# Five edits of order on TensorE, VectorE and ScalarE in a two-layer streaming trunk on one core

## The chip, the core and the metric

The kernel runs on one core of one Trainium2 chip. Its time is the device time of one execution in microseconds (us). Five engines of the core work side by side, each through its own list of instructions in order: TensorE (PE in the profile; its weight loads are shown apart as PEld), VectorE (DVE), ScalarE (ACT), GpSimd (POOL) and SyncE (SP). They wait for one another by semaphores that count up. A lower time is better.

## The reference, cut to what matters

The input is 512 frames of 1024 numbers. Layer 0 has two kinds of attention side by side, layer 1 a gated recurrence; behind each stands a feed-forward part with a convolution of width 3, and a last norm closes the trunk. Every input of a mixer or a feed-forward part is first normed and then shifted and scaled by vectors computed from the condition `c`.

```python
for l in range(DEPTH):                                  # DEPTH = 2
    mod = cond @ ada_w[l] + ada_b[l]
    sh1, sc1, g1, sh2, sc2, g2 = jnp.split(mod, 6, axis=-1)
    h = modulate(rms_norm(x, norm_mix_g[l]), sh1, sc1)
    y = stick_window_mixer(h, ...) if l % 2 == 0 else hgrn2_mixer(h, ...)
    x = x + g1[:, None, :] * y
    h = modulate(rms_norm(x, norm_ffn_g[l]), sh2, sc2)
    x = x + g2[:, None, :] * conv_ffn(h, ...)           # ((gelu(conv(h Wg))) * (h Wu)) Wd
return rms_norm(x, final_g)

# sliding-window heads of layer 0 (8 of them), per block of 128 queries:
m = max(max(logits), sink)
p = exp(logits - m)
out = (p / (sum(p) + exp(sink - m))) @ v
```

## The kernel before, in words

**Products in three parts.** The big products are made to float32 accuracy from parts of lower precision. Each operand is split into a high part (ACT rounds it: `w_hi`, `hT_hi`) and a low part (DVE subtracts: `w_lo`, `hT_lo`), and TensorE adds three matmuls in one PSUM bank: high weights by high input, high weights by low input, low weights by high input. A *unit* is a block of weights of 1024 columns: for each of the 8 chunks k of the input it has these three matmuls of 128x512, 24 in all. SP loads a unit into one of two slots, ACT and DVE split it, TensorE uses it (`unit`, line 1626).

**Pairs of units.** Behind a norm the chunks of the input come one by one, so the first two units behind it run as a pair (`unit_pair`, line 1648): chunk k of the first unit, and two chunks later (`LAG`) that of the second. The first unit waits at each chunk for `h_lo`, which DVE counts up when the chunk's low part is done; ACT counts `h_hi` for the high part. There are four such calls: the output projection of layer 0 (`U_OUT0`), the feed-forward parts of both layers (`U_FFN0`, `U_FFN1`) and the input projection of layer 1 (`U_IN1`). The last three stand right behind a norm, whose chunks DVE makes by lines 1056 (normed and scaled) and 1062 (low part) in turn, with ACT's line 653 (high part) between them.

**Opening.** The first four units run as a `quad` over half of the chunks, then over the other half. Between the two halves TensorE transposes columns of the input x (`x_columns`), makes the sums of the second half of the first condition vectors (`first_sums(1)`, 16 matmuls of one column), transposes two more columns, and issues four dummy matmuls whose result nobody reads (`keep_clock`).

**Window heads ("band heads").** The 8 sliding-window heads of layer 0 go through three pairs of PSUM banks in turn: `window_logits` (PE), `window_max` (DVE), `window_exp` (ACT), `window_norm` (DVE), `window_transposes` (PE), `window_copy` (the first bank of the pair by ACT, line 750, the second by DVE, line 1238), `window_values` (PE, into `obank`), `window_out` (DVE, line 1243, after each second head). ACT counts its copies in `pt_act`, DVE in `pt_dve`. Head 7's part of the loop also holds chunks 0 and 1 of the pair `U_OUT0`, which writes to the banks `proj`, the pair of banks of heads 0, 3 and 6.

**Second half of the last product.** `down(1)` makes the last product in two halves of 11 units. When the first half is out, DVE scales its columns (`final_scale`, line 1400), and TensorE transposes them (`final_transposes`, 16 transposes) behind the first unit of the second half; ACT copies one bank of them away (line 889). Eight units in a loop and two last ones (`last_two`) follow.

Everything here is set by the order in which the lines are written out; there is no scheduler. Two lines that decide a step below:

```python
1923                    window_values(h - 1)                                  # h = 7
1924                    unit_pair(U_OUT0, h_base["o0"], range(0, 2))
```

Of the kernel before, what the change touches and what calls it, by code (L numbers as in the profile page):

```python
# [31 lines left out]
P = 128  # L32
SEQ = 512
D = 1024
DC = D // P
# [52 lines left out]
U_OUT0 = U_IN0 + len(UNITS0)  # L88
# [7 lines left out]
HALF = FB // 2  # L96
# [62 lines left out]
def trunk(nc, x, c, ada_w, ada_b, norm_mix_g, norm_ffn_g, ab_w_in, ab_sinks, ab_w_out, hg_w_in,  # L159
          hg_lb_gamma, hg_onorm_g, hg_w_out, ffn_w_gate, ffn_w_up, ffn_conv_w, ffn_conv_b,  # L160
          ffn_w_down, final_g, tables, level_masks, out):
    with ExitStack() as ctx:
# [435 lines left out]
        def _(act):  # L598
# [8 lines left out]
            def split(u, slot):  # L607

                if isinstance(u, int) and u < 4:
                    act.wait_ge(raw_in[slot], 32 * (u // 2 + 1))  # L610
                else:
                    act.wait_ge(raw_in[slot], u * 8 + (48 - 8 * slot))
                if isinstance(u, int) and u < 4:
                    dst = (w_hi[:, slot, :], quad_hi[slot])[u // 2]
                else:
                    dst = w_hi[:, slot, :]
                    if isinstance(u, int) and u < 6:
                        act.wait_ge(quad_half, 1)
                    else:
                        act.wait_ge(unit_mm, u - 1)  # L620
                nc.scalar.activation(dst, w_raw[:, slot, :], ACT.Copy).then_inc(hi_done, 1)  # L621
# [256 lines left out]
            def down(u0, n, last=False):  # L878
                act.preload_act_table_set(EXP_LN_SET)
                with act.Fori(0, HALF // 2) as i:  # L880
                    for s in range(2):
                        split(u0 + 2 * i + (2 + s), s)
                for q in range(4):
                    squares(n, q)
                split(u0 + HALF + 1, 0)
                split(u0 + HALF + 2, 1)
                if last:
                    act.wait_ge(misc_full, MISC_AT["fin"] + 1)
                    nc.scalar.activation(out_nat[:, TB - 1, 0:512], misc[:], ACT.Copy).then_inc(misc_free, 1)
                with act.Fori(0, HALF // 2 - 1) as i:  # L890
                    for s in range(2):
                        split(u0 + HALF + 3 + 2 * i + s, s)
                for q in range(4, DC):
                    squares(n, q)
                if not last:
                    split(u0 + FB, 0)
                    split(u0 + FB + 1, 1)
                    root(n)
                    modulated(n)
# [107 lines left out]
        def _(dve):  # L1007
# [207 lines left out]
            def window_max(h):  # L1215
                s = h % 3
                for b in range(TB):
                    z, lo, _, n = window_block(b, s)
                    dve.wait_ge(sw_full, 2 * h + 1 + b // 2)
                    link(nc.vector.tensor_reduce(soft[:, s, 3, b:b + 1], z[:, lo:lo + n], AX.X, ALU.max))  # L1220
                nc.vector.tensor_scalar(soft[:, s, 0, :], soft[:, s, 3, :], sinks[:, h:h + 1], -1.0,
                                        ALU.max, ALU.mult).then_inc(max_done, 1)

            def window_norm(h):
                s = h % 3
                dve.wait_ge(p_done, h + 1)
                link(nc.vector.tensor_tensor(soft[:, s, 3, :], soft[:, s, 1, :], soft[:, s, 2, :], ALU.add))
                link(nc.vector.reciprocal(soft[:, s, 2, :], soft[:, s, 3, :]))
                for b in range(TB):
                    _, _, at, n = window_block(b, s)  # L1230
                    nc.vector.tensor_scalar(p_bufs[s][:, at:at + n], p_bufs[s][:, at:at + n],
                                            soft[:, s, 2, b:b + 1], None, ALU.mult).then_inc(p_norm, 1)

            def window_copy(h):
                dve.wait_ge(pt_full, 2 * h + 2)
                if h >= 3:
                    dve.wait_ge(pv_done, SB_HEADS + h - 2)
                nc.vector.tensor_copy(pt_bufs[h % 3][:, 384:896], pairs[h % 3][1][:]).then_inc(pt_dve, 1)
# [67 lines left out]


            window_norm(1)
            window_max(2)
            split(U_OUT0 + 1, 1)  # L1310
            window_copy(0)
            for h in range(1, SW_HEADS):
                window_copy(h)
                if h + 1 < SW_HEADS:
# [285 lines left out]
        def _(pe):  # L1600
# [50 lines left out]
            def unit_pair(u, h_from, ks=range(DC)):  # L1651


                parts_ready(u + 1)
                steps = [(k, 0) for k in ks] + [(k, 1) for k in ks]
                for k, s in sorted(steps, key=lambda step: step[0] + LAG * step[1]):
                    if s == 0:
                        pe.wait_ge(h_lo, h_from + k + 1)
                    at = slice(k * P, (k + 1) * P)
                    mm(proj[s][:], w_hi[:, s, at], hT_hi[:, k, :], start=(k == 0))  # L1660
                    mm(proj[s][:], w_hi[:, s, at], hT_lo[:, k, :])
                    last = mm(proj[s][:], w_lo[:, s, at], hT_hi[:, k, :], stop=(k == DC - 1))
                    if k == DC - 1:
                        last.then_inc(unit_mm, 1)
                    elif s == 0 and k == DC // 2 - 1:
                        last.then_inc(pair_half, 1)
# [120 lines left out]
            keep_clock(proj[0], 5)  # L1787
            quad(0)
            x_columns(range(3, 6))
            pe.wait_ge(first_used, 2 * DC)  # L1790
            misc_wait("first1")
            first_sums(1)
            x_columns(range(6, DC))
            pe.wait_ge(x_new, 6)
            keep_clock(zb[3], 4)

            def tile_in(b):

# [117 lines left out]
            for h in range(1, SW_HEADS):  # L1916
                if h < SW_HEADS - 1:
                    window_transposes(h)
                    window_values(h - 1)
                    if h + 2 < SW_HEADS:  # L1920
                        window_logits(h + 2)
                else:
                    window_values(h - 1)
                    unit_pair(U_OUT0, h_base["o0"], range(0, 2))
                    window_transposes(h)

            unit_pair(U_OUT0, h_base["o0"], range(2, 4))
# [31 lines left out]
            def down(layer, u0, n):  # L1959
# [64 lines left out]
                pe.wait_ge(gp_lo, FB * (layer + 1))  # L2024
                last_two(u0 + HALF - 2, 1, FB - 4, down_banks[0])
                one(u0 + HALF, 1, 0, first=True, mod_group=(8, None)[layer], banks=down_banks[1])
                if layer:
                    pe.wait_ge(fin_y, 4)
                    pe.wait_ge(gap_free, len(GAP_MODS))
                    misc_wait("fin")  # L2030
                    final_transposes(0, range(TB - 1), range(4)).then_inc(fin_full, 1)
                    final_transposes(0, range(TB - 1, TB), range(4)).then_inc(misc_full, 1)
                with pe.Fori(0, HALF // 2 - 1) as i:
                    for s in range(2):
                        one(u0 + HALF + 1 + 2 * i + s, s, 4 * i + 2 * s + 2, banks=down_banks[1])
                last_two(u0 + FB - 2, 0, FB - 4, down_banks[1])
                if not layer:
                    norm_sum(n)
# [124 lines left out]
```

## Time and profile before

| what | value |
|---|---|
| median of 3 runs | 1359.72 us (1358.35 to 1359.87) |
| the profiled execution, its own time | 1360.04 us |
| its span, first to last instruction | 1358.2 us |
| TensorE matmul busy in the span | 1323.5 us (97%) |
| TensorE weight loads busy | 1083.0 us (80%) |
| DVE, ACT, POOL busy | 808.7, 558.1, 46.9 us |
| mean granted TensorE clock | 0.993 |

The page gives one execution. Busy time is time in instructions; in a row of the timeline the bracket tells how long the engine had been idle before it and what released it. A row that ends in x4 stands for four instructions of the same kind in a run. PEclk is the granted TensorE clock as a share of 2.4 GHz: 1.00 or, at the lower of its two levels (1.2 GHz), 0.50.

### The profile page before, as it was taken

The numbers are of one execution on the slowest core, as the hardware profiler recorded it, in microseconds if no ns is written. First come the engines' busy times: TensorE is split into PE (matmuls) and PEld (weight loads), VectorE is DVE, ScalarE is ACT, GpSimd is POOL, SyncE is SP. The second block draws the span as 40 slices with busy tenths as digits, with TensorE's granted clock in tenths as the row PEclk, the third lists the DMA queues.
The fourth block names the chain that finished last, engine by engine and source line by source line (L and its number), as shares of the span: only waits on it lengthen the run. The fifth ranks groups of instructions, "written<-read, shape, count | busy, mean of one in ns | idle before, by whom it ended". The sixth has DMA issues, their size and how long they took to land.

```text
span 1358.2 us, 17432 instructions
## 1 busy us (share of the span) xinstructions
PE 1323.5 (97%) x6281; PEld 1083.0 (80%) x6281; DVE 808.7 (60%) x1197; ACT 558.1 (41%) x837; POOL 46.9 (3%) x92
## 2 busy tenths in 40 slices
PE   6999998899999999999999999999999999999998
PEld 5877776777888888888778888888788888888786
DVE  5745557567666656436697777775765455552423
ACT  6656554334333333212255555553343333332212
POOL 1000000000000000001100000000000000000000
PEclk9999999999999999999999999999999999999998
DMA  9543431153544555465622222224523333332232
GB/s 336 167 124 109 125 109 32 46 164 103 150 142 143 150 146 147 141 184 190 210 82 78 76 65 63 74 67 125 155 78 95 105 93 93 94 107 93 82 100 81
DMA packets 190148, 160.38 MB, mean 118 GB/s; under 512 B 5271, under 2 KB 163176, under 8 KB 190098
## 3 DMA queue, kind: packets, MB, share of 16 engines
q1 hardware_dynamic: 177696, 116.34, 28.5%
q0 software_dynamic: 11856, 42.68, 10.4%
q8 instruction: 32, 0.52, 0.2%
q10 hardware_dynamic: 546, 0.69, 0.1%
q14 instruction: 18, 0.15, 0.0%
HBM read 157.59 MB, written 2.10 MB: 118 GB/s over the span
## 4 chain that ended last, share of the span: by engine, by line
PE 89%; DVE 5%; ACT 2%; SPq 1%; issue 1%; DMA 1%; DVEq 0%; ACTq 0%
PE proj L1603 61%; PE z L1603 22%; PE obank L1603 3%; PE misc L1603 2%; SPq L479 1%; DVE ada_sum L1118 1%; DMA w_raw<-ab_w_in 1%; DVE normed L1056 0%; ACT w_hi L621 0%; DVE hT_lo L1062 0%; SPq L489 0%; DVE soft L1220 0%; ACT q_sb L741 0%; DVE w_lo L1018 0%; DVE xT L1410 0%
## 5 line engine op out<-in xcount | busy, mean ns | idle before, releaser
L1603 PE MATMUL proj<-hT_hi,w_hi 128*128 128x512 f32 x1112 | 441.5, 397 | 4.6 <-DVE hT_lo L1062 4.1
L1603 PE MATMUL proj<-hT_hi,w_lo 128*128 128x512 f32 x1112 | 433.7, 390 | 0.0
L1603 PE MATMUL proj<-hT_lo,w_hi 128*128 128x512 f32 x1112 | 433.4, 390 | 0.0
L1018 DVE TENSOR_TENSOR w_lo<-w_raw,w_hi 128x1024 fp32r<-128x1024 f32 x189 | 231.2, 1224 | 338.6 <-ACT w_hi L621 338.6
L621 ACT ACTIVATE w_hi<-w_raw 128x1024 fp32r<-128x1024 f32 x191 | 202.0, 1059 | 442.7 <-PE proj L1603 261.2
L1603 PEld LDWEIGHTS proj<-hT_hi,w_hi 128*128 128x128 f32 x1112 | 209.2, 188 | 57.2 <-DVE hT_lo L1062 8.0
L1603 PEld LDWEIGHTS proj<-hT_hi,w_lo 128*128 128x128 f32 x1112 | 209.0, 188 | 44.4
L1603 PEld LDWEIGHTS proj<-hT_lo,w_hi 128*128 128x128 f32 x1112 | 209.3, 188 | 43.3 <-issue 1.7
L1603 PE MATMUL z<-gated_hi,w_hi 128*128 (+1 forms) x264 | 104.5, 396 | 0.2 <-DVE xT L1410 0.2
L1603 PE MATMUL z<-gated_hi,w_lo 128*128 (+1 forms) x264 | 102.8, 389 | 0.0
L1603 PE MATMUL z<-gated_lo,w_hi 128*128 (+1 forms) x264 | 102.8, 389 | 0.0
L1165 DVE SCALAR_TENSOR_TENSOR ada_sum<-ada_raw,cond,ada_sum 128x1024 f32<-128x1024 f32 x70 | 89.6, 1280 | 2.5 <-DVE ada_sum L1165 0.5
L867 ACT ACTIVATE square<-square,small 128x512 f32<-128x512 f32 x44 | 31.9, 724 | 131.1 <-DVE square L1373 131.1
L567 POOL DMA_DIRECT2D ada_raw<-ada_w x80 | 42.4, 530 | 899.8 <-DVE ada_sum L1165 468.7
L1603 PEld LDWEIGHTS z<-gated_hi,w_hi 128*128 128x128 f32 x264 | 49.6, 188 | 10.4 <-DVE xT L1410 0.6
L1603 PEld LDWEIGHTS z<-gated_hi,w_lo 128*128 128x128 f32 x264 | 49.6, 188 | 10.4
L1603 PEld LDWEIGHTS z<-gated_lo,w_hi 128*128 128x128 f32 x264 | 49.6, 188 | 9.5
L1380 DVE TENSOR_TENSOR h<-proj,square 128x512 f32<-128x512 f32 x44 | 30.4, 691 | 23.6 <-PE proj L1603 22.4
L639 ACT ACTIVATE square<-xT 128x512 f32<-128x512 f32 x28 | 17.7, 632 | 52.0 <-DVE xT L1335 32.0
L1286 DVE SCALAR_TENSOR_TENSOR soft_a<-z,soft_a 128x128 f32<-128x128 f32 (+3 forms) x32 | 13.5, 483 | 37.3 <-ACT soft_a L800 37.3
L1373 DVE SCALAR_TENSOR_TENSOR square<-normed,small,square 128x512 f32<-128x512 f32 x44 | 33.1, 752 | 3.9 <-DVE square L1369 0.2
L1369 DVE SCALAR_TENSOR_TENSOR square<-normed,small,square 128x512 f32<-128x512 f32 x44 | 33.0, 751 | 3.9 <-DVE square L1366 0.2
(326 smaller groups left out, 1620.6 us busy)
## 6 DMA issues: line engine op xcount, KB each, us to landing
ada_raw<-ada_w POOLq DMA_DIRECT2D x80, 512.0 KB, 4.3
w_raw<-ffn_w_gate SPq DMA_DIRECT2D x44, 512.0 KB, 3.8
w_raw<-ffn_w_up SPq DMA_DIRECT2D x44, 512.0 KB, 3.9
w_raw<-ffn_w_down SPq DMA_DIRECT2D x44, 512.0 KB, 3.4
w_raw<-hg_w_in SPq DMA_DIRECT2D x32, 512.0 KB, 4.1
ada_first<-ada_w SPq DMA_DIRECT2D x16, 512.0 KB, 10.9
w_raw<-ab_w_in SPq DMA_DIRECT2D x14, 512.0 KB, 5.0
w_raw<-ab_w_out SPq DMA_DIRECT2D x8, 512.0 KB, 4.4
```

What stands on the lines that cost most here:

```text
L479: sp.dma_start(ada_first[:, DC * (1 - h) + k, :].rearrange("p (g n) -> p g n", g=2), src).then_inc(ada_first_in[h][k], 16)
L567: pool.dma_start(ada_raw[:, m % ADA_SLOTS, :], ada_w[layer].rearrange("(p k) n -> p k n", k=DC)[:, k, which * D:(which + 1) * D]).then_inc ...
L621: nc.scalar.activation(dst, w_raw[:, slot, :], ACT.Copy).then_inc(hi_done, 1)
L639: nc.scalar.activation(dst, xT[:, dc, :], ACT.Square).then_inc(sq_done, 1)
L867: nc.scalar.activation(square[:, 1, :], square[:, 0, :], ACT.Gelu_apprx_tanh, bias=conv_col(layer, 3, f)).then_inc(gelu_done, 1)
L1018: nc.vector.tensor_tensor(w_lo[:, slot, :], w_raw[:, slot, :], w_hi[:, slot, :].bitcast(F32), ALU.subtract).then_inc(lo_done, 1)
L1118: nc.vector.scalar_tensor_tensor(out=acc, in0=raw, scalar=scale, in1=acc, op0=ALU.mult, op1=ALU.add).then_inc(first_used, 1)
L1165: nc.vector.scalar_tensor_tensor(out=acc, in0=raw, scalar=scale, in1=acc, op0=ALU.mult, op1=ALU.add).then_inc(ada_used, 1)
L1369: nc.vector.scalar_tensor_tensor(out=square[:, 0, :], in0=normed[:, 0, 1:1 + SEQ], scalar=conv_col(layer, 1, f), in1=square[:, 0, :], op0= ...
L1373: nc.vector.scalar_tensor_tensor(out=square[:, 0, :], in0=normed[:, 0, 2:2 + SEQ], scalar=conv_col(layer, 2, f), in1=square[:, 0, :], op0= ...
L1380: nc.vector.tensor_tensor(h32[:, 0, :], proj[1][:], square[:, 1, :], ALU.mult).then_inc(gp_done, 1)
L1603: return nc.tensor.matmul(dst, weights_ap, moving, start=start, stop=stop, skip_group_check=True)
```

## The change

Five edits, all of them of order or of waits; no instruction is new but two dummy matmuls in the opening, and four dummies there go.

```diff
@@ ScalarE, down(): ACT's copy of the transposed bank goes behind the splits of the loop
+                with act.Fori(0, HALF // 2 - 1) as i:
+                    for s in range(2):
+                        split(u0 + HALF + 3 + 2 * i + s, s)
                 if last:
                     act.wait_ge(misc_full, MISC_AT["fin"] + 1)
                     nc.scalar.activation(out_nat[:, TB - 1, 0:512], misc[:], ACT.Copy).then_inc(misc_free, 1)
-                with act.Fori(0, HALF // 2 - 1) as i:
-                    for s in range(2):
-                        split(u0 + HALF + 3 + 2 * i + s, s)
@@ VectorE, window heads
             window_norm(1)
+            window_copy(0)
             window_max(2)
             split(U_OUT0 + 1, 1)
-            window_copy(0)
@@ TensorE, unit_pair()
+                    at = slice(k * P, (k + 1) * P)
+                    if s == 0:
+                        pe.wait_ge(h_hi, h_from + k + 1)
+                    mm(proj[s][:], w_hi[:, s, at], hT_hi[:, k, :], start=(k == 0))
+                    mm(proj[s][:], w_lo[:, s, at], hT_hi[:, k, :])
                     if s == 0:
                         pe.wait_ge(h_lo, h_from + k + 1)
-                    at = slice(k * P, (k + 1) * P)
-                    mm(proj[s][:], w_hi[:, s, at], hT_hi[:, k, :], start=(k == 0))
-                    mm(proj[s][:], w_hi[:, s, at], hT_lo[:, k, :])
-                    last = mm(proj[s][:], w_lo[:, s, at], hT_hi[:, k, :], stop=(k == DC - 1))
+                    last = mm(proj[s][:], w_hi[:, s, at], hT_lo[:, k, :], stop=(k == DC - 1))
@@ TensorE, opening
+            misc_wait("first1")
+            keep_clock(misc, 2)
             pe.wait_ge(first_used, 2 * DC)
-            misc_wait("first1")
             first_sums(1)
             x_columns(range(6, DC))
-            pe.wait_ge(x_new, 6)
-            keep_clock(zb[3], 4)
@@ TensorE, window heads, h = 7
+                    pe.wait_ge(pt_act, h)
+                    pe.wait_ge(pt_dve, h)
+                    unit_pair(U_OUT0, h_base["o0"], range(0, 2))
                     window_values(h - 1)
-                    unit_pair(U_OUT0, h_base["o0"], range(0, 2))
                     window_transposes(h)
@@ TensorE, down(): the loop goes ahead of the final transposes
+                with pe.Fori(0, HALF // 2 - 1) as i:
+                    for s in range(2):
+                        one(u0 + HALF + 1 + 2 * i + s, s, 4 * i + 2 * s + 2, banks=down_banks[1])
                 if layer:
                     pe.wait_ge(fin_y, 4)
                     pe.wait_ge(gap_free, len(GAP_MODS))
                     misc_wait("fin")
                     final_transposes(0, range(TB - 1), range(4)).then_inc(fin_full, 1)
                     final_transposes(0, range(TB - 1, TB), range(4)).then_inc(misc_full, 1)
-                with pe.Fori(0, HALF // 2 - 1) as i:
-                    for s in range(2):
-                        one(u0 + HALF + 1 + 2 * i + s, s, 4 * i + 2 * s + 2, banks=down_banks[1])
```

TensorE's row between the two halves of the opening quad (`z<-table,x_nat` are the transposes of x, `misc<-table,ada_sum` the one-column sums, `slope_r,ident_r` the dummies):

```order
-L1706 MATMUL z<-table,x_nat 128x128 x12
+L1708 MATMUL z<-table,x_nat 128x128 x12
+L1603 MATMUL misc<-slope_r,ident_r 128x512 x2
 L1603 MATMUL misc<-table,ada_sum 128x1 x8
-L1706 MATMUL z<-table,x_nat 128x128 x8
-L1603 MATMUL z<-slope_r,ident_r 128x512 x4
+L1708 MATMUL z<-table,x_nat 128x128 x8
 L1603 MATMUL z<-hT_hi,quad_w 128x512
```

Two dummies stand ahead of the sums, none ahead of the quad's second half.

VectorE's row where the window heads begin (the scalings of head 1, the copy of head 0 out of `proj`, the maxima of head 2, the split of a unit, the copy of head 1):

```order
 L1231 TENSOR_SCALAR soft_a<-soft_a,soft 128x128
 L1231 TENSOR_SCALAR soft_a<-soft_a,soft 128x256 x3
+L1238 COPY k_sb<-proj 128x512
 L1220 TENSOR_REDUCE soft<-z 128x1 x4
 L1221 TENSOR_SCALAR soft<-soft,sinks 128x4
 L1018 TENSOR_TENSOR w_lo<-w_raw,w_hi 128x1024
-L1238 COPY k_sb<-proj 128x512
 L1238 COPY pt_pair<-z 128x512
```

The copy of head 0 has gone ahead of four reductions, their maximum and one split.

TensorE's row at head 7, before (transposes of head 6, values of heads 5 and 6, chunks 0 and 1 of the pair, transposes of head 7):

```order
L1831 MATMUL proj<-table,q_sb 128x128 x7
L1603 MATMUL obank<-pt_pair,v_nat 64x128 x7
L1603 MATMUL obank<-k_sb,v_nat 64x128 x7
L1603 MATMUL proj<-hT_hi,w_hi 128x512
L1603 MATMUL proj<-hT_lo,w_hi 128x512
L1603 MATMUL proj<-hT_hi,w_lo 128x512
...
L1831 MATMUL z<-table,soft_a 128x128 x7
```

And now:

```order
L1832 MATMUL proj<-table,q_sb 128x128 x7
L1603 MATMUL obank<-pt_pair,v_nat 64x128 x7
L1603 MATMUL proj<-hT_hi,w_hi 128x512
L1603 MATMUL proj<-hT_hi,w_lo 128x512
L1603 MATMUL proj<-hT_lo,w_hi 128x512
...
L1603 MATMUL obank<-k_sb,v_nat 64x128 x7
L1832 MATMUL z<-table,soft_a 128x128 x7
```

The 12 matmuls of the pair have gone ahead of the values of head 6, and within each three the one with `hT_lo` is last.

## Rows read from the trace of the kernel before

**Rows 1.** The page: busy time and share of the span; then the chain's shares.

```profile
PE 1323.5 (97%) x6281; PEld 1083.0 (80%) x6281; DVE 808.7 (60%) x1197; ACT 558.1 (41%) x837; POOL 46.9 (3%) x92
PE 89%; DVE 5%; ACT 2%; SPq 1%; issue 1%; DMA 1%; DVEq 0%; ACTq 0%
```

**Rows 2.** Windows, 40 us of steady units: window, length, busy (instructions) per engine, PEclk, DMA.

```profile
320.00:360.00 40.00, 40.00 (x179) 33.10 (x178) 26.14 (x33) 15.29 (x20) 2.12 (x4) 1.00 0.55 158
```

**Rows 3.** Timeline of PE and ACT in the opening: start, us, instruction, [idle before].

```profile
41.03 1.95 PE L1603 MATMUL misc<-table,ada_sum 128*128 128x1 f32 x16 [0.53 <-DVE ada_sum L1118]
43.41 0.81 ACT L705 ACTIVATE hT_hi<-x_hat,mod,scale_g 128x512 fp32r<-128x512 f32 x1 [0.30 <-DVE scale_g L1129]
44.37 2.06 PE L1603 MATMUL z<-slope_r,ident_r 128*128 128x512 f32 x4
46.23 0.46 PE L1603 MATMUL z<-hT_hi,quad_w 128*128 128x512 f32 x1
```

**Rows 4.** Windows at both levels of the clock, columns as in rows 2.

```profile
18.00:22.00 4.00, 4.00 (x39) 4.00 (x38) 3.71 (x3) 3.87 (x8) 0.00 (x0) 1.00 1.09 360
43.00:46.00 3.00, 3.00 (x12) 2.71 (x12) 2.56 (x5) 2.70 (x5) 0.00 (x0) 0.50 0.61 175
...
218.00:246.00 28.00, 21.53 (x145) 17.59 (x143) 21.91 (x65) 14.56 (x55) 0.00 (x0) 1.00 0.00 1
248.00:251.00 3.00, 3.00 (x9) 2.23 (x8) 0.00 (x0) 0.00 (x0) 0.00 (x0) 0.50 0.00 0
```

**Rows 5.** Timeline of DVE, ACT and PE at the first window heads.

```profile
208.79 1.66 DVE L1220 TENSOR_REDUCE soft<-z 128x1 f32<-128x128 f32 x4
...
211.76 0.68 DVE L1238 COPY k_sb<-proj 128x512 f32<-128x512 f32 x1
...
212.46 0.30 ACT L743 ACTIVATE soft<-soft,sinks 128x4 f32<-128x4 f32 x1
...
212.54 2.23 PE L1603 MATMUL obank<-k_sb,v_nat 128*64 128x128 f32 x14 [2.63 <-issue]
...
212.96 0.15 DVE L1227 TENSOR_TENSOR soft<-soft 128x4 f32<-128x4 f32 x1
...
216.70 0.75 DVE L1220 TENSOR_REDUCE soft<-proj 128x1 f32<-128x128 f32 x2 [2.27 <-PE proj L1603]
...
219.27 0.37 ACT L741 ACTIVATE q_sb<-proj,soft 128x128 f32<-128x128 f32 x1 [5.61 <-DVE soft L1221]
```

**Rows 6.** Timeline of ACT and PE at heads 6 and 7.

```profile
243.97 0.49 ACT L750 ACTIVATE k_sb<-proj 128x384 f32<-128x384 f32 x1
...
246.35 1.91 PE L1603 MATMUL obank<-k_sb,v_nat 128*64 128x128 f32 x14 [3.44 <-DVE oT L1243]
248.20 0.80 PE L1603 MATMUL proj<-hT_hi,w_hi 128*128 128x512 f32 x1
...
252.41 0.93 PE L1831 MATMUL z<-table,soft_a 128*128 128x128 f32 x7
```

**Rows 7.** Waits of PE: engine line, waited for, us in total, times, longest.

```profile
PE proj L1603 <- DVE hT_lo L1062: 4.1, 9, 0.8
```

**Rows 8.** Timeline of ACT, DVE and PE, chunk 2 of the pair U_FFN0.

```profile
306.81 0.72 ACT L653 ACTIVATE hT_hi<-normed,mod 128x512 fp32r<-128x512 f32 x1 [0.94 <-DVE normed L1056]
...
308.14 0.75 DVE L1062 SCALAR_TENSOR_TENSOR hT_lo<-normed,mod,hT_hi 128x512 fp32r<-128x512 f32 x1
...
308.94 0.50 PE L1603 MATMUL proj<-hT_hi,w_hi 128*128 128x512 f32 x1 [0.49 <-DVE hT_lo L1062]
```

**Rows 9.** Timeline of DVE and PE between the halves of down(1).

```profile
1287.10 1.23 DVE L1018 TENSOR_TENSOR w_lo<-w_raw,w_hi 128x1024 fp32r<-128x1024 f32 x1 [0.26 <-ACT w_hi L621]
...
1287.52 0.39 PE L1603 MATMUL z<-gated_hi,w_lo 128*128 128x512 f32 x1
...
1289.96 1.09 PE L2013 MATMUL z<-table,ada_raw 128*128 128x128 f32 x8 [2.05 <-DVE ada_raw L1400]
```

## The prediction

> **What bounds the kernel now.** I read the page's busy times and the chain of waits first, then the list of what TensorE waited for, then the timeline around each idle stretch of TensorE. The reader is to see that one engine carries the end: TensorE is busy 1323.5 of 1358.2 us, and the chain that ended last runs 89% through it [rows 1]. In a steady stretch it has no idle time at all: 40.00 of 40.00 us, and with 177 matmuls in it a matmul of 128x512 takes 40 / 177 = 0.226 us from start to start [rows 2]. So the time is the work of TensorE plus its gaps, and a gap that is closed shifts all that comes behind, as long as the other engines' work behind it hangs on TensorE too. From 254 us to the end it does: the weights are split two units ahead, and the only gaps that are left are the short ones named below.
>
> The Trainium skill ("Perfetto Trace Analysis", section "Identifying the Most-Contended Engine") says that matmul busy time is a poor measure for TensorE and that the busy share of its weight loads should be read instead. By that rule the page's 80% [rows 1] would leave a fifth of the engine free, and closed gaps could turn up again elsewhere. The trace doesn't bear this out here: in the stretch without any gap the loads are busy 33.10 of 40.00 us, 83% [rows 2], so some 80% is what a full TensorE shows in this kernel.
>
> The sum is made against the profiled execution, 1360.04 us (its span of 1358.2 and 1.84 around it). It lies 0.3 above the median of the runs, 1359.72, which is less than those three differ among themselves.
>
> **Opening.** TensorE comes to the dummies at 44.37, and the quad's second half starts at 46.23 [rows 3]. It needs the first high part of the new chunks, which ACT has ready at 43.41 + 0.81 = 44.22 [rows 3]. Without the dummies the quad starts at about 44.3: 1.93 earlier. The next parts are in time: after 12 matmuls (2.7 us) it would want the next low part at 47.0, and DVE makes it in the order of before. The two new dummies stand where TensorE was idle for 0.53 us before the sums [rows 3]; two at 0.226 are 0.45, so they cost nothing. What is unsure is the clock. It was at 0.50 from 43 to 46 [rows 4]: before that TensorE had done 12 transposes, idled 0.53 and then worked on one-column sums. If the two dummies keep it at 1.00, the gain is the whole 1.9. If it falls as before, the quad starts at about 44.4, but its first four or five matmuls go at half the pace; by 46.25 it has done (46.25 - 44.4) / 0.43 = 4.3 of them, worth 4.3 x 0.226 = 1.0. So the term is 1.0 to 1.9. For 1.9 speaks that the stretch from 18 to 22, nearly all transposes, kept 1.00 [rows 4], so transposes did not bring it down there, and the gap before the sums is what the dummies fill. I take 1.9.
>
> **First window heads.** TensorE idled 2.63 us until 212.54 [rows 5]. The values of head 0 needed both copies of head 0. ACT's was long done; DVE's stood behind the maxima and the split and began at 211.76. Moved ahead, it runs at 208.79 to 209.47, and the values start where TensorE stops, at 209.9. That gap closes, but the gain is what the next wait leaves. The maxima of head 2 now start 0.60 later (a copy is 0.68 long and 0.60 from start to start: two of them fill 211.76 to 212.96 [rows 5]), so the exponentials end at 212.46 + 0.60 + 0.30 = 213.4 and the scaling of head 2 starts there, against 212.96 [rows 5]. It lasts 1.4 (0.15 for the row at 212.96, 0.18 and 1.07 for the two steps behind it). Then come the maxima of head 3, at 214.8, for which TensorE's logits are now ready (209.9 + 1.7 values + some 2.2 logits = 213.8). Before, they started at 216.70, after DVE had idled 2.27 for them, and went slowly, since TensorE was at half clock: ACT's exponentials of head 3 followed at 219.27 [rows 5]. At the pace of the maxima of head 2 (1.83 with the last step: the 2.97 from 208.79 to 211.76 [rows 5] less the split's 1.14) they follow at 214.8 + 1.83 + 0.13 = 216.8. Gain: 2.5. From here to head 6 each head goes round through exponentials, scaling and maxima (ACT and DVE), and TensorE waits 0.3 to 1.2 per head; that ring keeps its pace, so the 2.5 stays. The bounds: if the low parts of the ring hid all of it, 0; if the closed gap counted in full with the half clock behind it, 2.63 + 1.5 = 4.1. The rows of the ring speak for 2.5.
>
> **Head 7.** The values of head 6 waited until DVE had emptied `obank`: 3.44 us idle, to 246.35 [rows 6]. Now the pair's 12 matmuls go there. They wait for the copies of head 6, since they write to its banks; ACT's copy ends at 243.97 + 0.49 = 244.46 [rows 6], so they start at 244.55 (times as before). What is queued behind that new wait is the values and the transposes of head 6 and 7, and these could not start before 246.3 anyway. 12 x 0.226 = 2.7 brings 247.3; values 1.7, so the transposes of head 7 start at 249.0 instead of 252.41 [rows 6]. Gain: 3.4, of which 1.8 is wait and 1.6 is the clock: it stood at 0.50 from 248 to 251 [rows 4], and the same 12 matmuls took 252.41 - 248.20 = 4.2 us. That part hangs on the gap that is left being short enough: TensorE stops at 246.35 - 3.44 = 242.91, so it is 244.55 - 242.91 = 1.6 us. Gaps of up to 1.2 between 218 and 246 left the clock at 1.00 [rows 4]; those of 2.63 and 3.44 were followed by 0.50. 1.6 is nearer to 1.2. Term: 1.8 to 3.4, I take 3.4.
>
> **Pairs.** Behind the three norms TensorE waits for the low part of a chunk, 9 times, 4.1 us in total [rows 7]. At chunk 2 of `U_FFN0` the high part is done at 306.81 + 0.72 = 307.5, the low part at 308.14 + 0.75 = 308.9, and TensorE starts at 308.94 [rows 8]. Chunks come every 1.45 us (DVE's two instructions of 0.75), TensorE needs 6 x 0.226 = 1.36 for one, so it is held by DVE up to chunk 6. With both high products first, two of the three matmuls are done when the low part lands; at the last chunk that holds TensorE, two matmuls fewer are left: 2 x 0.226 = 0.45 per pair. It is not 4.1 us, because DVE's pace stays and only the lead changes. Three pairs: 1.3 (bounds: 0, if the wait for the high part takes its place, and 4.1). The pair `U_OUT0` has no such waits and gains nothing.
>
> **Last product.** TensorE's last matmul ahead of the transposes starts at 1287.52, so it could go on at 1287.75. It waited for DVE's scalings until 1289.96 [rows 9]. Now the next unit comes first, whose low weights are ready at 1287.10 + 1.23 = 1288.33; start 1288.45. The transposes themselves (1.7 us) are only moved. Gain: 1289.96 - 1288.45 = 1.5; bounds 0 and 2.2. ACT's copy, behind the splits, is done long before `misc` is used again at the end.
>
> **Sum.** 1.9 + 2.5 + 3.4 + 1.3 + 1.5 = 10.6; 1360.04 - 10.6 = 1349.4 us.
>
> **Rivals.**
> 1. *The clock falls again in one place*, in the opening (0.9 less) or at head 7 (1.6 less). For: all three low stretches of the trace followed thin or idle work, and at both places some is left. Against: rows 4, as said. Time: 1350.3, 1351.0, or 1351.9 for both.
> 2. *The order changes less than it says.* The ring of the window heads takes back the 2.5 and the high-first order earns nothing, because the wait for high parts is as late as that for low ones. For: DVE was 60% busy and is in both. Against: high parts are 1.4 us ahead in rows 8, and DVE idled 2.27 in rows 5. Time: 1349.4 + 3.8 = 1353.2; with the 1.9 of the opening spent on a later wait too, 1355.1.
> 3. *Everything is given back*: closed gaps open again at a wait that does not hang on TensorE, a weight transfer above all. Against: none of TensorE's waits in the whole trace behind 10 us is for a transfer. Time: 1358 to 1360.
> 4. *Slower: the pairs run at half clock.* The place is the three pairs behind the norms, where TensorE now works in small bits between two kinds of waits. At 0.50 the 48 matmuls of a pair take 48 x 0.43 = 20.6 us instead of 12.8 (6 chunks at 1.45 up to the last that holds it, and 18 matmuls at 0.226 from there), 7.8 more; in all three, 23.5 more, which with the other gains of 9.3 gives 1374.2. It decides from the point where two pairs run wholly at 0.50. Against: the pairs are at 1.00 now with the same waits, and no low stretch of rows 4 outlasted 4 us.
>
> **Chances.** My forecast 0.47; rival 1 0.27; rival 2 0.11; rival 3 0.05; rival 4 0.03; the rest, 0.07, for a time below 1348.5, if the fall of the clock goes in more places than I counted. A difference below 0.2%, 2.7 us, can't be told from no change here; faster means below 1357.0. Faster: 0.47 + 0.27 + 0.11 + 0.07 = 0.92; within 0.2%: 0.05; slower: 0.03. The range reaches from 1347.5 (the forecast, less the spread of the runs of before, 1.5, and a little) to 1353.5, which takes in rival 1 and the first time of rival 2; the likeliest case alone has 1348.4 to 1350.2.
>
> **What would show it.** Right: no dummies between the transposes and the quad, and the quad about 1.9 earlier with a clock of 1.00 at 43 to 46; no gap ahead of the values of head 0 and a first exponential of head 3 about 4.4 us earlier than 219.27; a gap of about 1.6 ahead of the pair at head 7; in a pair, the waits for the low part now ahead of the third matmul, and the pair 0.45 shorter from the first high part's time; about 0.7 idle ahead of the loop in the last product. Wrong: a clock of 0.50 where it was 1.00, waits on `hT_hi` as long as those on `hT_lo` were, or a first wait of TensorE for a transfer.

## The result, and the profile after

The changed kernel took 1351.28 us in the median of 4 runs (1349.70 to 1352.02), the kernel before 1359.80 beside it (1358.35 to 1361.47). The ratio is 0.9937, 95% interval 0.9923 to 0.9952. It is faster by 8.5 us; forecast were 1349.4 us and 10.6. The profiled execution of the changed kernel took 1349.70 us, 10.3 less than the profiled one of before (1360.04), and was the fastest of the four.

The page of the changed kernel, its busy times and the shares of the chain of waits:

```profile
PE 1317.6 (98%) x6279; PEld 1077.6 (80%) x6279; DVE 808.9 (60%) x1197; ACT 558.2 (41%) x837; POOL 46.8 (3%) x92
PE 89%; DVE 5%; ACT 3%; SPq 1%; issue 1%; DMA 1%; DVEq 0%; ACTq 0%
```

The bound is the same as before [rows 1]: TensorE, 1317.6 of a span of 1347.9 us. Its busy time itself fell by 5.9 us (1323.5 before [rows 1]) which a closed wait can't do; 0.45 of it are the two dummies less, the rest is the clock. Windows over the three places where the clock had stood low, columns as in rows 2: first the one of the kernel before that rows 4 leave out, then three of the changed kernel:

```profile
213.00:217.00 4.00, 4.00 (x19) 3.39 (x18) 1.65 (x8) 0.66 (x2) 0.00 (x0) 0.57 0.46 135
```

```profile
43.00:46.00 3.00, 2.63 (x16) 2.08 (x15) 2.56 (x6) 2.92 (x5) 0.00 (x0) 1.00 0.59 175
213.00:217.00 4.00, 4.00 (x29) 3.53 (x30) 2.36 (x7) 2.22 (x10) 0.00 (x0) 1.00 0.19 58
248.00:251.00 3.00, 3.00 (x20) 2.36 (x19) 0.69 (x1) 0.16 (x1) 0.00 (x0) 1.00 0.00 0
```

All three are at 1.00 (2.4 GHz), where they were at 0.50, 0.57 and 0.50 [rows 4 and the row above]; 0.50 is 1.2 GHz. Now the timeline of TensorE and ScalarE at the places of the prediction: opening, first window heads, head 7, a pair, last product (start, us, instruction, [idle before]):

```profile
38.91 1.47 PE L1708 MATMUL z<-table,x_nat 128*128 128x128 f32 x12
40.14 0.71 PE L1603 MATMUL misc<-slope_r,ident_r 128*128 128x512 f32 x2
40.95 1.95 PE L1603 MATMUL misc<-table,ada_sum 128*128 128x1 f32 x16
42.76 1.07 PE L1708 MATMUL z<-table,x_nat 128*128 128x128 f32 x8
44.20 0.50 PE L1603 MATMUL z<-hT_hi,quad_w 128*128 128x512 f32 x1 [0.37 <-ACT hT_hi L705]
...
207.87 1.74 PE L1603 MATMUL obank<-k_sb,v_nat 128*64 128x128 f32 x14
218.36 0.98 PE L1832 MATMUL proj<-table,q_sb 128*128 128x128 f32 x7 [0.63 <-DVE q_sb L1231]
...
239.49 0.50 ACT L750 ACTIVATE k_sb<-proj 128x384 f32<-128x384 f32 x1
240.04 0.50 PE L1603 MATMUL proj<-hT_hi,w_hi 128*128 128x512 f32 x1 [1.61 <-ACT k_sb L750]
242.99 1.74 PE L1603 MATMUL obank<-k_sb,v_nat 128*64 128x128 f32 x14
244.66 0.98 PE L1832 MATMUL z<-table,soft_a 128*128 128x128 f32 x7
...
299.14 0.72 ACT L653 ACTIVATE hT_hi<-normed,mod 128x512 fp32r<-128x512 f32 x1 [0.94 <-DVE normed L1056]
299.82 0.50 PE L1603 MATMUL proj<-hT_lo,w_hi 128*128 128x512 f32 x1 [0.48 <-DVE hT_lo L1062]
...
1279.67 0.49 PE L1603 MATMUL proj<-gated_hi,w_hi 128*128 x1 [0.58 <-DVE w_lo L1018]
```

The quad's second half starts 2.0 earlier than in rows 3. The values of head 0 have no gap ahead of them, where rows 5 have 2.63. At head 7 the pair's 12 matmuls now stand ahead of head 6's values, and TensorE waits 1.61 for ScalarE's copy ahead of them, where it waited 3.44 for `obank` [rows 6]. In the pair the wait is now at the low part's product. Ahead of the last loop the idle time is 0.58 instead of 2.05 [rows 9]. The waits of TensorE that have to do with the pairs (engine line, waited for, us in total, times, longest):

```profile
PE proj L1603 <- DVE hT_lo L1062: 2.9, 6, 0.5
...
PE proj L1603 <- ACT q_hg L968: 0.7, 1, 0.7
```

Rows 7 had 4.1 us in 9 waits. The second row is where one pair gives back 0.2 of its 0.45: before, that wait was 0.48.

### The profile page after: what moved, and what is told of

It is laid out like the page before. It is cut to its first block, busy times and chain, and to the rows that moved or that the text cites. A ratio compares the mean times of both kernels' runs of the same rounds, so it can differ in the third digit from the quotient of the medians.

```text
span 1347.9 us, 17428 instructions
## 1 busy us (share of the span) xinstructions
PE 1317.6 (98%) x6279; PEld 1077.6 (80%) x6279; DVE 808.9 (60%) x1197; ACT 558.2 (41%) x837; POOL 46.8 (3%) x92
## 4 chain that ended last, share of the span: by engine, by line
PE 89%; DVE 5%; ACT 3%; SPq 1%; issue 1%; DMA 1%; DVEq 0%; ACTq 0%
PE proj L1603 60%; PE z L1603 22%; PE obank L1603 3%; PE misc L1603 2%; DVE normed L1056 1%; DVE hT_lo L1062 1%; SPq L479 1%; DVE ada_sum L1118 1%; DVE soft L1220 1%; DMA w_raw<-ab_w_in 1%; ACT w_hi L621 0%; SPq L489 0%; ACT q_sb L741 0%; DVE w_lo L1018 0%; DVE xT L1410 0%
## 5 line engine op out<-in xcount | busy, mean ns | idle before, releaser
L1603 PE MATMUL proj<-gated_hi,w_hi 128*128 (+1 forms) x88 | 35.0, 397 | 0.6 <-DVE w_lo L1018 0.6
L1373 DVE SCALAR_TENSOR_TENSOR square<-normed,small,square 128x512 f32<-128x512 f32 x44 | 33.1, 752 | 3.9 <-DVE square L1369 0.2
```

The lines of the kernel that those rows point to most:

```text
L1373: nc.vector.scalar_tensor_tensor(out=square[:, 0, :], in0=normed[:, 0, 2:2 + SEQ], scalar=conv_col(layer, 2, f), in1=square[:, 0, :], op0= ...
L1603: return nc.tensor.matmul(dst, weights_ap, moving, start=start, stop=stop, skip_group_check=True)
```

## The experiments

Each kernel was timed in 5 runs beside the kernel before, whose median was 1359.9 each time (1357.8 to 1361.8 in 27 runs). The nine runs of the changed kernel, the first four and the five below, have a median of 1351.26 us (1349.70 to 1352.10), to which the medians of the others are compared. Differences below 1 us between two such medians are not told apart, and where the ranges overlap widely even 1.5 us is not certain from five runs. In all but the first the diff is against the changed kernel.

**The changed kernel again.** No edit.

> The changed kernel once more, for its spread. In the profiled execution it took 1349.70 us at a granted clock of 0.999, in three others 1351.3 to 1352.0 at 0.997 to 0.998. Theory (the clock falls in some executions, at a place where the profiled one shows none): the times lie again between 1349.7 and 1352, longer where the mean clock of a run is lower, and a profile of a run above 1351 shows a stretch at half clock ahead of 250 us. Rival (the work itself differs by run, waits or transfers): a profile of a run above 1351 shows full clock up to 1345 us, and longer idle time of TensorE.

1350.75 us (1349.80 to 1352.10), ratio 0.9931 [0.9917, 0.9945]. Its five runs, with the mean granted clock: 1349.80 (0.999), 1349.89 (0.998), 1350.75 (0.998), 1351.98 (0.997), 1352.10 (0.997). The last is the profiled one. Its timeline, then its window (columns as in rows 2):

```profile
27.92 0.79 PE L1603 MATMUL z<-hT_hi,w_hi 128*128 128x512 f32 x1 [0.61 <-ACT hT_hi L705]
...
41.74 1.48 PE L1708 MATMUL z<-table,x_nat 128*128 128x128 f32 x12
...
46.66 0.50 PE L1603 MATMUL z<-hT_hi,quad_w 128*128 128x512 f32 x1 [0.37 <-ACT hT_hi L705]
```

```profile
28.00:34.00 6.00, 6.00 (x14) 4.71 (x15) 6.00 (x8) 5.59 (x9) 0.00 (x0) 0.51 1.04 385
```

The theory holds: the quad's first half runs at 1.2 GHz (0.51), and its second half starts 2.46 us later than in the first profile. The whole trace is 2.4 us longer (1350.3 against 1347.9), so that is all of it. In the trace of before this stretch was at 1.00, and so it was in the first profile after.

**The opening as before.**

```
 x_columns(range(3, 6))
+pe.wait_ge(first_used, 2 * DC)
 misc_wait("first1")
-keep_clock(misc, 2)
-pe.wait_ge(first_used, 2 * DC)
 first_sums(1)
 x_columns(range(6, DC))
+pe.wait_ge(x_new, 6)
+keep_clock(zb[3], 4)
```

> The changed kernel with the opening as before (second sums behind the wait for the sixth squares and ahead of it no dummies, four dummies behind the last sums' columns). Theory: the opening earned 1.98 us, so first attention head's logits begin near 57.3 us again, the clock at 43 to 46 us is 0.50, and the time is about 1351.7 in the profiled execution, ratio of medians to the changed kernel 1.001 to 1.0015. Rival (only the 0.9 us of clock was earned in most executions, or it comes back at head 0): the time is within 1.0 us of the changed kernel's.

1351.58 us (1351.54 to 1351.80), ratio 0.9938 [0.9925, 0.9952]: only 0.3 above the changed kernel, so the rival holds. Its timeline of TensorE and two windows:

```profile
39.92 1.47 PE L1708 MATMUL z<-table,x_nat 128*128 128x128 f32 x12
41.23 1.84 PE L1603 MATMUL misc<-table,ada_sum 128*128 128x1 f32 x16
42.94 1.07 PE L1708 MATMUL z<-table,x_nat 128*128 128x128 f32 x8
43.76 1.17 PE L1603 MATMUL z<-slope_r,ident_r 128*128 128x512 f32 x4
44.77 0.39 PE L1603 MATMUL z<-hT_hi,quad_w 128*128 128x512 f32 x1
```

```profile
28.00:34.00 6.00, 6.00 (x22) 4.84 (x21) 6.00 (x8) 5.10 (x9) 0.00 (x0) 0.78 1.05 387
43.00:46.00 3.00, 3.00 (x19) 2.62 (x19) 2.45 (x5) 2.67 (x5) 0.00 (x0) 1.00 0.61 175
690.00:700.00 10.00, 9.31 (x43) 7.74 (x42) 9.26 (x17) 6.13 (x8) 0.00 (x0) 0.83 0.21 60
```

Here the clock fell at 28 and had risen again by 43. TensorE came to the sums late enough not to wait for them, and the old order took 44.77 - 39.92 = 4.85 us from the transposes to the quad's second half. The new order took 46.66 - 41.74 = 4.92 in the run above and 5.29 in the first profile; in the trace of before the old one, with the clock at 0.50, ended at 46.23 [rows 3]. So the 1.9 of the opening is nearly all clock, and by these traces it is there only where the clock falls at 43 with the old order and not with the new.

**Head 7 as before** (values of head 6 first).

```
-pe.wait_ge(pt_act, h)
-pe.wait_ge(pt_dve, h)
-unit_pair(U_OUT0, h_base["o0"], range(0, 2))
 window_values(h - 1)
+unit_pair(U_OUT0, h_base["o0"], range(0, 2))
```

> The changed kernel with the old order at head 7 (values of head 6 first, then the first two steps of the pair). Theory: 3.3 us are lost, 1.65 of them as a longer wait of the values for the two copies and 1.6 as a stretch at half clock behind it: about 1353.0 us profiled. Rival (the clock falls at head 7 in the changed kernel as well in most executions, so the edit earns just the wait): 1.7 us lost in the median.

1354.00 us (1352.55 to 1355.58), ratio 0.9955 [0.9940, 0.9970]: 2.7 lost. Timeline of TensorE:

```profile
241.82 3.22 PE L1603 MATMUL obank<-k_sb,v_nat 128*64 128x128 f32 x14 [3.44 <-DVE oT L1243]
244.96 0.80 PE L1603 MATMUL proj<-hT_hi,w_hi 128*128 128x512 f32 x1
...
248.97 0.93 PE L1832 MATMUL z<-table,soft_a 128*128 128x128 f32 x7
```

The wait of 3.44 is that of before. The transposes of head 7 come 4.3 us later than at 244.66, more than the 3.3 expected, since in this execution the clock was low already in the values (3.22 us for what takes 1.74). The part that the clock takes here is 1.6 to 2.6.

**The pairs as before.**

```
-mm(proj[s][:], w_lo[:, s, at], hT_hi[:, k, :])
-if s == 0:
-    pe.wait_ge(h_lo, h_from + k + 1)
-last = mm(proj[s][:], w_hi[:, s, at], hT_lo[:, k, :], stop=(k == DC - 1))
+mm(proj[s][:], w_hi[:, s, at], hT_lo[:, k, :])
+last = mm(proj[s][:], w_lo[:, s, at], hT_hi[:, k, :], stop=(k == DC - 1))
```

In front of the three the wait is for `h_lo` instead of `h_hi`.

> The changed kernel with the old order in the pairs (low part of the input second, wait for it ahead of the first matmul). Theory: each pair behind a norm loses one matmul less a restart, 0.45 us, of which the third pair had already given back 0.2: about 1.15 us lost, 1350.85 profiled, and the pair at head 7 loses nothing. Rival (the waits for the low part are only moved and cost a restart each): within 0.3 us of the changed kernel.

1352.61 us (1350.81 to 1353.04), ratio 0.9941 [0.9926, 0.9955]: 1.35 lost in the median, with ranges that overlap. The profiled execution is the one of 1352.61, not the 1350.85 expected, since its clock stood low from 26 to 33; that delay is in the trace before the pairs and is left out here. By the trace the pairs lose 0.44 up to 608 us and 0.70 from there to the last product, 1.14, as expected. (In the kernel before, `unit` begins at line 1636 and `unit_pair` at line 1651.)

**VectorE's copy as before**: `window_copy(0)` behind `window_max(2)` and the split.

> The changed kernel with VectorE's copy of head 0's transposed probabilities behind the maximum of head 2 and the split, as before. Theory: the values of head 0 wait 2.6 us longer and the first exponential of head 3 starts 2.5 us later: 1352.2 us profiled. Rival (later heads wait for VectorE anyway, and the time is made up within the heads): less than 1 us lost by head 7.

1352.81 us (1350.53 to 1354.69), ratio 0.9944 [0.9930, 0.9957]: 1.55 lost. Timeline of TensorE:

```profile
211.03 3.14 PE L1603 MATMUL obank<-k_sb,v_nat 128*64 128x128 f32 x14 [2.63 <-issue]
...
221.16 0.98 PE L1832 MATMUL proj<-table,q_sb 128*128 128x128 f32 x7 [0.32 <-DVE q_sb L1231]
```

In this trace the term is 2.3 up to head 7, as the theory has it. The gap of 2.63 is back, and the values behind it take 3.14 instead of 1.74. Where no clock fell (the run of 1350.53, at 0.999), only 0.8 was lost against 1349.70. That points to 0.8 for the wait itself and the rest for the clock; it rests on one run, and under 1 us is what the rival said.

**The last transposes as before**: `final_transposes(0, ...)` and ScalarE's copy ahead of the loop.

> The changed kernel with the final transposes of the first half of the output ahead of the last loop again (ScalarE's copy too). Theory: 1.5 us lost, all of it as idle time of TensorE ahead of the transposes at 1279 us; 1351.2 us profiled. Rival (the transposes at the end delay the last output instead, so that the old place costs less): under 0.7 us lost.

1353.62 us (1351.07 to 1354.52), ratio 0.9946 [0.9932, 0.9959]: 2.4 lost; 1.4 in its run at 0.999. Timeline of TensorE, then the window around it:

```profile
1282.80 1.97 PE L2016 MATMUL z<-table,ada_raw 128*128 128x128 f32 x8 [2.06 <-DVE ada_raw L1400]
```

```profile
1278.00:1290.00 12.00, 9.94 (x46) 8.46 (x45) 5.52 (x9) 3.24 (x4) 0.00 (x0) 0.86 0.26 90
```

The 2.05 of rows 9 is back as 2.06, and here the clock fell behind them, which it had not done in the trace of before. From the last wait of the last pair to the tail this trace takes 366.3 us, the changed kernel 363.1.

**Dummies at head 7.** `keep_clock(zb[3], 6)` ahead of the two waits in front of the pair.

> The changed kernel with six 128x512 dummy products (1.36 us) in the 1.61 us gap ahead of the pair at head 7; they write a bank that nothing reads. Theory (in the longer executions the clock falls behind this gap): the times draw together near 1349.7 us, median 1 to 1.6 us below the changed kernel's. Rival (the clock falls elsewhere, or what differs is not the clock at all): same median and same spread as the changed kernel, and the pair begins at 240.04 us as there.

1351.60 us (1349.65 to 1351.86), ratio 0.9936 [0.9923, 0.9950]: the rival, nothing gained. Its profile (1349.65 us) shows 1.00 up to the tail, and at this place so do the eight profiles that have the gap of 1.61: the clock does not fall behind it.

**Head 6's copies first.** On ScalarE `window_copy(6)` ahead of `window_exp(7)`, on VectorE ahead of `window_max(7)`.

> The changed kernel with both copies of head 6's transposed probabilities moved ahead: ScalarE's ahead of head 7's exponentials, VectorE's ahead of head 7's maxima. Theory: the pair at head 7 waits for these copies alone, so the gap of 1.61 us goes and the pair starts at 238.4 us; head 7's probabilities come 0.7 us later and still in time (about 242 us against transposes at 243 us): 1348.1 us profiled, 1.6 below the changed kernel. Rival (head 7's chain becomes the end: maxima, exponentials and weights of head 7 come later than the pair's end): under 0.8 us gained, the rest is a new gap ahead of the transposes of head 7.

1352.65 us (1350.20 to 1354.02), ratio 0.9941 [0.9927, 0.9954]: nothing gained, the gap moved. Timeline of VectorE and TensorE:

```profile
239.10 0.50 PE L1609 MATMUL proj<-hT_hi,w_hi 128*128 128x512 f32 x1
...
243.54 0.68 DVE L1246 COPY oT<-obank 128x512 f32<-128x512 f32 x1
...
244.37 3.22 PE L1609 MATMUL obank<-k_sb,v_nat 128*64 128x128 f32 x14 [2.24 <-DVE oT L1246]
```

The pair starts without a gap, but the values of head 6 wait 2.24 us for VectorE to empty `obank`. On VectorE that stands behind the weights of head 7. Neither theory had named it. The clock fell behind the 2.24, and in this run at 698 and at 43 as well, although the opening is that of the changed kernel:

```profile
43.00:46.00 3.00, 2.69 (x8) 1.90 (x7) 2.57 (x4) 3.00 (x6) 0.00 (x0) 0.50 0.52 154
```

From the transposes of x to those of head 6 this trace takes 1.3 us more than the changed kernel's first (38.33 to 236.51 against 38.91 to 235.78).

**Seven dummies at 27.** `keep_clock(proj[0], 7)` instead of 5 ahead of `quad(0)`.

> The changed kernel with seven dummies instead of five ahead of the first matmuls of the quad at 27.4 us, so that 0.45 of the 0.66 us gap there is filled. Theory (in the longer executions the clock falls in this gap): the profile shows 1.00 at 28 to 34 us, the times gather near 1349.7 us and the median is 1 us or more below the changed kernel's 1350.8 to 1351.3. Rival (the fall does not hang on this gap: it comes all the same, there or at one of the next gaps, 44 or 695 us): the same median and the same spread of 2.3 us.

1351.34 us (1349.99 to 1352.93), ratio 0.9940 [0.9926, 0.9953]: the rival. Timeline of TensorE, then two windows:

```profile
25.19 2.23 PE L1603 MATMUL proj<-slope_r,ident_r 128*128 128x512 f32 x7
27.27 0.80 PE L1603 MATMUL z<-hT_hi,w_hi 128*128 128x512 f32 x1
```

```profile
28.00:34.00 6.00, 6.00 (x24) 4.86 (x23) 6.00 (x9) 5.01 (x8) 0.00 (x0) 0.84 1.05 386
690.00:700.00 10.00, 9.30 (x43) 7.73 (x42) 9.26 (x17) 6.13 (x8) 0.00 (x0) 0.83 0.19 53
```

The clock falls within the dummies (2.23 us for seven), with no gap behind them; ahead of them stand 16 one-column sums. So it doesn't hang on the gap at 27. The wait that goes with it lies further ahead, at 17 us; see what stays open.

**Seven dummies, and the opening as before.** Both edits together.

> The same seven dummies, but with the opening's order as before. Theory: with the clock up at 27 us the old order pays each time for what it paid in the trace of before, 0.53 us of waiting and a stretch at half clock at 43 to 46 us, so it is 1.9 us slower than the kernel with seven dummies, where without them the two orders were 0.3 to 0.8 apart in the median. Rival (the opening's order is worth under 1 us in any case): within 1 us.

1351.51 us (1349.70 to 1351.80), ratio 0.9933 [0.9920, 0.9947]: within 0.2 of the one above. With the first opening experiment this makes two pairs of medians, 0.3 and 0.2 apart, for a term forecast at 1.9.

**Head 7 put right.** As the experiment with head 6's copies, but on VectorE in this order:

```
 window_norm(6); window_max(7)
+window_copy(6)
 low(3)
-window_copy(6)
+window_out(5)
 window_norm(7)
-window_out(5)
```

> The changed kernel with head 6's two copies ahead of head 7's exponentials (ScalarE) and of the low part (VectorE), as in the experiment that moved them, and with VectorE's emptying of the output bank (head 5) now ahead of the weights of head 7 as well. Theory (in that experiment the values of head 6 were held by that emptying, 2.24 us, so that the gap only moved): the pair starts right behind the values of head 5, the values of head 6 right behind the pair, and 1.6 us are earned against the changed kernel in runs of equal clock: 1348.1 us at a mean clock of 0.999. Rival (head 7's transposes become the end and wait for its weights): the transposes of head 7 wait 0.5 us or more, under 1 us earned.

1349.69 us (1349.53 to 1351.66), ratio 0.9931 [0.9917, 0.9944]. Timeline of ScalarE, VectorE and TensorE:

```profile
236.36 0.49 ACT L750 ACTIVATE k_sb<-proj 128x384 f32<-128x384 f32 x1 [1.26 <-PE proj L1840]
237.47 0.68 DVE L1241 COPY k_sb<-proj 128x512 f32<-128x512 f32 x1
238.36 0.50 PE L1611 MATMUL proj<-hT_hi,w_hi 128*128 128x512 f32 x1
238.67 0.68 DVE L1246 COPY oT<-obank 128x512 f32<-128x512 f32 x1
241.31 1.74 PE L1611 MATMUL obank<-k_sb,v_nat 128*64 128x128 f32 x14
242.98 0.98 PE L1840 MATMUL z<-table,soft_a 128*128 128x128 f32 x7
```

The transposes of head 7 start 1.68 earlier than at 244.66, with no gap left. The profiled run (1349.66 at 0.997) had the clock at 0.83 from 690 to 700, which took 1.5 of it back. The theory holds in the trace: all three starts came as said, and the rival's wait of 0.5 isn't there. Its median is 1.6 below the changed kernel's nine runs, but its fastest run is only 0.2 below theirs, and 1348.1 was not reached: none of the five runs had a mean clock above 0.998. The gain in the time is likely, not shown.

**With more dummies on top** of the last: seven at 27, one at 44 (behind a wait for the sixth column, as in the old opening), two in the recurrent layer at 693 (`mm(zb[3][:], ones, sumsq[:], True, True)`).

> The same as the last, with seven dummies ahead of the quad, one ahead of its second half at 44 us and two ahead of the third unit of the recurrent layer at 695 us. Theory: no stretch at half clock ahead of the tail, 1348.0 us and a spread under 1 us. Rival (the clock falls behind another gap): a stretch at half clock elsewhere, and a median above 1349 us.

1349.93 us (1349.14 to 1350.52), ratio 0.9928 [0.9914, 0.9942]. Not told apart from the last in the median; the spread is 1.4 instead of 2.1. The clock was at 0.80 from 40 to 45, so the rival holds. Timeline of TensorE at the third place:

```profile
693.50 1.96 PE L1611 MATMUL z<-sumsq,table 128*128 128x512 f32 x4
694.90 0.79 PE L1611 MATMUL proj<-hT_hi,w_hi 128*128 128x512 f32 x1
```

These two dummies are stored as four instructions, and the next unit starts 1.40 us behind their start, where two dummies of the other kind take 0.45; they fill the gap of 0.7 and push the next unit back by 0.6 us more.

## Why the prediction was right in the trace and 1.9 us too low in the median

Each term, as forecast and as measured. "In the traces" is before against after; "undone" is what the kernel without that edit lost: in its trace, in its best run against 1349.70, and in its median against 1351.26. The rows are rounded; 10.3 is the difference of the spans.

| term | forecast | in the traces | undone: trace | best run | median |
|---|---|---|---|---|---|
| Opening | 1.9 | 2.0 | 0 | 1.8 | 0.3 |
| First window heads | 2.5 | 2.5 | 2.3 | 0.8 | 1.6 |
| Head 7 | 3.4 | 3.3 | 4.3 | 2.9 | 2.7 |
| Pairs | 1.3 | 1.1 | 1.1 | 1.1 | 1.4 |
| Last product | 1.5 | 1.5 | 3.2 | 1.4 | 2.4 |
| sum | 10.6 | 10.3 | | | 8.4 |

**Opening.** The step that failed, by 1.6 us in the median, where 2.1 are missing in all (8.5 for 10.6). It was forecast at 1.9, with bounds of 1.0 and 1.9, from one trace: the dummies go and the clock stays up. Both came true in the first profile. But the trace of before showed one of two courses of this stretch. If the clock falls at 28 instead, it is up again at 43, the sums are not waited for, and the old order is as quick as the new (4.85 against 4.92). Even the lower bound took it for given that the clock was up at 28. The clock fell at 28 in 7 of the 13 profiles with the new kernel or a variant of it, which fits a term of 0.3 in the median. Nor do the two new dummies always hold the clock: of the six profiles with the new order and no fall at 28, two fell at 43 (head 6's copies first; the last experiment, with one more dummy). The 1.8 in the table's best run is no measure, since none of the five runs was free of a fall; with seven dummies, the best runs were 1349.99 for the new order and 1349.70 for the old.

**First window heads, head 7, last product.** The order did what was said, and each wait was of the forecast size. What varies from run to run is what the clock adds behind the old gap, so that the terms come out between 0.8 and 2.5, 2.7 and 4.3, 1.4 and 3.2. The bounds of the first (0 to 4.1) hold that; those of head 7 (1.8 to 3.4) and of the last product (0 to 2.2) ended too low. That the 1.61 left at head 7 would keep the clock up was right, in every profile with that gap.

**Pairs.** Right in place and size. One pair of three gave 0.2 back to a wait for ScalarE's `q_hg`, 0.70 at 694.78.

**The rivals.** The first, the clock falling again, came true in most of the profiles, but mostly at other places than named. In the 13 it fell at 26 to 34 in 7, at 694 to 703 in 7, at 43 to 46, a place that was named, in 2, and at head 7, the other, only where its gap was 2.24 or 3.44. (It also fell in each undone kernel at the gap that came back: 2.63 at the first window heads, 2.06 ahead of the last transposes.) The fall at 695 costs 1.5 us each time (from the last wait of that pair at 677 to the last of the next at 975: 298.2 without, 299.7 with it). Neither 27 nor 695 was low in the trace of before, so the prediction had no row for them. The mechanism's time, 1350.3 to 1351.9, is what was measured; its place was not. The rivals that the order earns less, that all is given back, or that the pairs run at half clock found nothing for them in the traces. One reservation: the wait at 695, 0.70 in the changed kernel, is one that the edit of the pairs made longer. With the old pairs it is:

```profile
697.20 0.50 PE L1603 MATMUL proj<-hT_hi,w_hi 128*128 128x512 f32 x1 [0.48 <-ACT q_hg L968]
```

Where it was 0.65 to 0.72, the clock fell in 7 of 11 profiles; in the two where it was 0.48 (before, and the old pairs) and in the one where dummies filled it, the clock stayed up. Three profiles are too few to tell. If the edit brings this fall, it pays 1.5 us in those executions for the 1.1 that it earns, although the median with the old pairs was no better.

The Trainium skill ("Perfetto Trace Analysis", section "Identifying the Most-Contended Engine") judges the room on TensorE by the busy share of its weight loads (beside the share of peak), and would read the free fifth as room. Their share is 80% before and after, while ten microseconds of gaps and low clock went and none came back; so in this kernel that share is no sign of room.

**What stays open.** What decides in which execution the clock falls at 27. One thing goes with it without exception: in the 7 profiles where it fell there, TensorE had idled 0.50 to 0.95 us at 17 us, behind the 20 dummies of the start and ahead of transposes that need a result of ScalarE; the other 6, and the trace of before, have no such wait. This is the run of the changed kernel in which the clock fell:

```profile
10.13 6.35 PE L1603 MATMUL z<-slope_r,ident_r 128*128 128x512 f32 x20
17.19 0.52 PE L1780 MATMUL z<-table,ada_raw 128*128 128x128 f32 x3 [0.71 <-ACT ada_sum L693]
```

The 20 dummies took 5.97 to 6.35 us where the clock fell later, and 6.74 to 7.41 where it did not: where they are done early, TensorE waits. So it goes with the start of the execution, not with an edit. That the wait at 17 causes the fall at 27 is not shown, and why the dummies differ in pace isn't either; the profiles show a granted clock of 1.00 for them. More dummies at the start, enough to close that wait, would test it; no run did. Whether the kernel before has the same falls at 27 and 695 is open too, since only one of its executions was profiled. Its 27 runs beside these kernels spread over 4.0 us and their mean clock over 0.991 to 0.996, so its falls vary too, but not at which place.

## What to carry to other kernels

Split every gap's price into the wait and the low clock behind it, and forecast the second as a chance, from several profiles if they can be had: one trace shows one course. Undo each edit of a change by itself and compare medians; edits upstream of each other can pay for the same microsecond. When a wait is moved, follow what the next instruction waits for: the copies at head 6 earned nothing until the emptying of the output bank went ahead with them.

## What the runs showed that was not expected

- Between executions of one binary the clock of TensorE falls at different places, at 27 or not, at 695 or not, and the runs lie up to 2.4 us apart (1349.70 to 1352.10); the one fall at 27 that was profiled in the changed kernel accounts for all of its 2.4.
- A gap of 0.7 us at 695 was followed by 1.2 GHz in 7 of 11 profiles, and at 26 the clock fell within a run of dummies with no gap next to it; behind the gap of 1.61 at head 7 it never fell, in eight profiles.
- An idle time of 0.50 to 0.95 us at 17 us stood in all 7 profiles whose clock fell at 26 to 28, and in none of the others.
- A 128x512 product with float32 operands ones and sumsq took 0.70 us from start to start (1.40 for two) and is stored as two instructions, against 0.226 for those of the big products (type fp32r in the rows).
